# Pairwise-added squares ahead of the norm sums, a separate PSUM bank for the last row block, and a later weight split in a five-layer kernel

## What is computed

```
for each layer:
    h = modulate(rmsnorm(x, g0), sh1, sc1)
    x = x + g1 * mixer(h)              # swa, gla, fox, swa, and a mixed attention ("b2") last
    h = modulate(rmsnorm(x, g1_), sh2, sc2)
    x = x + g2 * feed_forward(h)       # width 2816; with a convolution in the last layer
rmsnorm(x, g) = x * rsqrt(mean(x * x) + 1e-6) * g
```

## Time and profile before

| | |
|---|---|
| median of 3 runs | 1724.33 us (1722.63 to 1727.8) |
| the profiled execution's own time | 1730.59 us |
| its span, first to last instruction | 1728.8 us |
| TensorE matmul busy | 1604.8 us, 93% |
| VectorE busy | 1199.9 us, 69% |
| ScalarE busy | 788.2 us, 46% |
| GpSimd busy | 87.8 us, 5% |
| mean granted TensorE clock | 0.972 |

### The profile page before, as it was taken

How to read it: one execution, slowest core, us unless ns; L and a number is a source line. 1 busy time by engine, 2 the same in 40 slices (tenths; PEclk the granted TensorE clock), 3 DMA queues, 4 the chain that set the end, 5 groups by cost and what they waited for, 6 DMA issues and landing times.

```text
span 1728.8 us, 30748 instructions
## 1 busy us (share of the span) xinstructions
PE 1604.8 (93%) x12542; PEld 1524.9 (88%) x12542; DVE 1199.9 (69%) x1592; ACT 788.2 (46%) x1030; POOL 87.8 (5%) x105
## 2 busy tenths in 40 slices
PE   0878999999899999999999999879999989999998
PEld 0767999999789999998899999858999989889998
DVE  4897777776557777775377777856877778566665
ACT  1453433345534343444454344545434467755453
POOL 0032000000000000001100000020000002300000
PEclk9988999999889999999999999999999999999999
DMA  8755488855324978762339876422987745345550
GB/s 327 301 209 209 199 338 310 321 201 181 116 76 197 385 292 315 267 220 100 144 124 387 307 298 244 183 98 98 365 315 291 295 138 176 123 151 180 185 181 33
DMA packets 54219, 383.75 MB, mean 222 GB/s; under 512 B 6256, under 2 KB 6512, under 8 KB 8448
## 3 DMA queue, kind: packets, MB, share of 16 engines
q1 hardware_dynamic: 50400, 363.75, 56.0%
q0 software_dynamic: 3744, 18.94, 3.1%
HBM read 378.47 MB, written 4.19 MB: 221 GB/s over the span
## 4 chain that ended last, share of the span: by engine, by line
PE 86%; DVE 8%; DMA 2%; ACT 2%; issue 1%; POOL 1%; SPq 0%; DVEq 0%; ACTq 0%
PE PS L1647 71%; PE PS L1668 4%; PE PS L1694 2%; DVE wlo L1173 2%; PE PS L1767 2%; DMA adar<-ada 2%; DVE adar L1187 1%; PE PS L1793 1%; ACT whi L779 1%; DVE XN L1225 1%; PE PS L1814 1%; DVE NM L1330 1%; DVE SCR L1324 1%; DMA raw<-weights 1%; PE PS L1770 1%
## 5 line engine op out<-in xcount | busy, mean ns | idle before, releaser
L1647 PE MATMUL PS<-hhi,whi 128*128 128x256 f32 x2568 | 744.2, 290 | 26.6 <-DVE hlo L1218 23.5
L1647 PE MATMUL PS<-hlo,whi 128*128 128x256 f32 x2568 | 735.8, 287 | 0.0
L1173 DVE TENSOR_TENSOR wlo<-raw,whi 128x2048 fp32r<-128x2048 f32 x234 | 537.0, 2295 | 286.2 <-ACT whi L779 286.1
L1647 PE MATMUL PS<-hhi,wlo 128*128 128x256 f32 x2568 | 735.2, 286 | 0.0
L779 ACT ACTIVATE whi<-raw 128x2048 fp32r<-128x2048 f32 x234 | 446.5, 1911 | 509.8 <-PE PS L1647 481.8
L1647 PEld LDWEIGHTS PS<-hhi,whi 128*128 128x128 f32 x2568 | 502.8, 196 | 43.7 <-issue 40.2
L1647 PEld LDWEIGHTS PS<-hlo,whi 128*128 128x128 f32 x2568 | 503.1, 196 | 1.3 <-issue 1.2
L1647 PEld LDWEIGHTS PS<-hhi,wlo 128*128 128x128 f32 x2568 | 502.3, 196 | 0.0
L1187 DVE CUSTOM_DVE_ANT_0 adar<-adar,CB 128x1024 f32<-128x1024 f32 x240 | 286.4, 1233 | 13.4 <-DMA adar<-ada 13.3
L1647 PE MATMUL PS<-ahi,whi 128*128 128x256 f32 x936 | 265.9, 284 | 1.1 <-DVE alo L1605 1.1
L1647 PE MATMUL PS<-alo,whi 128*128 128x256 f32 x936 | 265.4, 284 | 0.0
(11 more groups left out here) (214 smaller groups left out, 1343.3 us busy)
## 6 DMA issues: line engine op xcount, KB each, us to landing
raw<-weights SPq DMA_DIRECT2D x234, 1024.0 KB, 6.3
adar<-ada SPq DMA_DIRECT2D x108, 1024.0 KB, 5.8
adar<-ada POOLq DMA_DIRECT2D x12, 1024.0 KB, 5.9
bias_rows<-acc POOLq DMA_DIRECT2D x12, 256.0 KB, 3.0
adar<-bias_rows POOLq DMA_DIRECT2D x8, 256.0 KB, 3.3
CST<-cst_in SPq DMA_DIRECT2D x1, 1128.0 KB, 11.7
CB<-c_in SPq DMA_DIRECT2D x2, 512.0 KB, 4.4
X<-x_in SPq DMA_DIRECT2D x1, 1024.0 KB, 8.1
```

The lines of the kernel that those rows point to most:

```text
L1173: v.tensor_tensor(wlo[:, u % CV, :], raw[:, u % RAW, :], whi[:, u % CV, :].bitcast(F32), ALU.subtract).then_inc(lo_done, 1)
L1647: m = pe.matmul(o, w(a), h(b), start=first and k_ == 0, stop=last and k_ == 2, skip_group_check=True)
```

## The change

It does four things. (1) ScalarE squares in five instructions, of two, two, two, one and one row blocks, and the norm's semaphore counts five per norm. (2) After a mixer and after a feed-forward part VectorE adds squares before TensorE sums them: after a mixer five additions put row blocks 0 to 5 into one, and TensorE sums 3 blocks (0, 6, 7); after a feed-forward part three additions put pairs together, and it sums 5 (0, 2, 6, 4, 7). (3) The last row block goes to bank 2, and a signal for block 6 is given before block 7 is multiplied (`out_half` in the out stage, a fourth `y_done` in `down`). Bank 2 is zeroed as a fifth bank before the feed-forward loop. (4) After a feed-forward part `lo` of the next layer's second unit stands behind the updates of x and the additions. In the out stage the splits and ScalarE's three `hi` keep their places; the additions stand between them. The two other norms only get the five squares.

The diff, without the bookkeeping of which norm stands where and the passing of the bank to the out matmuls:

```diff
@@ -250,6 +257,20 @@
         def mixer_ada(l):
             return range(LOOP_ADA[l - 1] + STEPS, LOOP_ADA[l]) if l else range(4, LOOP_ADA[0])
+
+        SQUARES = ((0, 2), (2, 2), (4, 2), (6, 1), (7, 1))
+
+        def adds_to(n):
+
+            return sum({"ffn": 3, "out": 5}.get(plan.place[m], 0) for m in range(n))
+
+        def down_bank(c):
+
+            return bank[4 + c // 2][:, S * (c % 2):S * (c % 2) + S] if c < C - 1 else bank[2][:, 0:S]
+
+        def out_bank(i, t):
+
+            return bank[2][:, 0:S] if (i, t) == (OUT_UNITS - 1, 1) else bank[IB[i]][:, S * t:S * t + S]
         def more_b2(l):
@@ -788,12 +809,12 @@
             def norm(n, l=None, which=0):
-                for q in range(4):
+                for k, w in SQUARES:
                     if n == 0:
                         act.wait_ge(x_in_s, 16)
                     else:
-                        act.wait_ge(x_ready, 8 * (n - 1) + 2 * q + 2)
-                    act.activation(XN[:, 2 * q:2 * q + 2, :], X[:, 2 * q:2 * q + 2, :], ACT.Square).then_inc(norm_sq, 1)
+                        act.wait_ge(x_ready, 8 * (n - 1) + k + w)
+                    act.activation(XN[:, k:k + w, :], X[:, k:k + w, :], ACT.Square).then_inc(norm_sq, 1)
                 act.wait_ge(norm_sum, n + 1)
                 root(RB[:, 0, :], RB[:, 1, :], bank[3][:, 0:S], D).then_inc(norm_r, 1)
                 if n != plan.final_norm:
@@ -1208,6 +1229,17 @@
                                        op0=ALU.add, op1=ALU.mult).then_inc(aff_s, 1)
                 v.wait_ge(aff_s, 2 * l + which + 1)
+            added = [0]
+
+            def add_squares(n, a, b, group=None):
+
+                if group:
+                    v.wait_ge(norm_sq, 5 * n + group)
+                else:
+                    v.wait_ge(norm_add, added[0])
+                added[0] += 1
+                v.tensor_tensor(XN[:, a, :], XN[:, a, :], XN[:, b, :], ALU.add).then_inc(norm_add, 1)
+
             def norm(n, l=None, which=0):
@@ -1559,13 +1591,27 @@
                         lo(plan.uout[l] + i + 2)
                     if l == 0 and i == 0:
                         ada_read(9)
-                    v.wait_ge(pe_unit, plan.uout[l] + i + 1)
+                    if i == OUT_UNITS - 1:
+                        add_squares(plan.norm[l] + 1, 4, 5, 3)
+                        add_squares(plan.norm[l] + 1, 0, 4)
+                    else:
+                        v.wait_ge(pe_unit, plan.uout[l] + i + 1)
                     if i == 0:
                         v.wait_ge(ada_mod, ADA_UNITS * l + 5 + 1)
                     for t in range(2):
                         k = 2 * i + t
-                        v.scalar_tensor_tensor(out=X[:, k, :], in0=bank[IB[i]][:, S * t:S * t + S], scalar=MOD[:, 48 * l + 16 + k:48 * l + 17 + k], in1=X[:, k, :],
+                        if i == OUT_UNITS - 1:
+                            if t == 0:
+                                v.wait_ge(out_half, l + 1)
+                            else:
+                                v.wait_ge(pe_unit, plan.uout[l] + i + 1)
+                        v.scalar_tensor_tensor(out=X[:, k, :], in0=out_bank(i, t), scalar=MOD[:, 48 * l + 16 + k:48 * l + 17 + k], in1=X[:, k, :],
                                                op0=ALU.mult, op1=ALU.add).then_inc(x_ready, 1)
+                    if i == 1:
+                        add_squares(plan.norm[l] + 1, 0, 1, 1)
+                    elif i == 2:
+                        add_squares(plan.norm[l] + 1, 2, 3, 2)
+                        add_squares(plan.norm[l] + 1, 0, 2)
                 affine(l, 1)
                 norm(plan.norm[l] + 1, l, 1)
@@ -1627,16 +1673,24 @@
                         act_lo(1 + st, add=i)
                         if more:
                             ada_add(a0 + st + 2 * i, st, 4 * a0 + 4 * st + 8 * i)
-                if more:
-                    lo(plan.uin[l + 1] + 1)
+                n = plan.norm[l + 1] - (kinds[l + 1] == "b2") if more else None
                 for k in range(8):
                     if k < 6:
-                        v.wait_ge(y_done, 3 * l + k // 2 + 1)
+                        v.wait_ge(y_done, 4 * l + k // 2 + 1)
+                    elif k == 6:
+                        v.wait_ge(y_done, 4 * l + 4)
                     else:
                         v.wait_ge(pe_unit, f + FFN_UNITS)
-                    v.scalar_tensor_tensor(out=X[:, k, :], in0=bank[4 + k // 2][:, S * (k % 2):S * (k % 2) + S], scalar=MOD[:, 48 * l + 40 + k:48 * l + 41 + k],
+                    v.scalar_tensor_tensor(out=X[:, k, :], in0=down_bank(k), scalar=MOD[:, 48 * l + 40 + k:48 * l + 41 + k],
                                            in1=X[:, k, :], op0=ALU.mult, op1=ALU.add).then_inc(x_ready, 1)
+                    if more and k == 3:
+                        add_squares(n, 0, 1, 1)
+                    elif more and k == 5:
+                        add_squares(n, 2, 3, 2)
+                if more:
+                    add_squares(n, 4, 5, 3)
+                    lo(plan.uin[l + 1] + 1)
         @block.tensor
@@ -1668,6 +1722,8 @@
                                 m = pe.matmul(o, hs[x][:, c, P * t:P * t + P], wt(a), start=(c == 0 and k_ == 0), stop=(c == C - 1 and k_ == 2))
                         else:
                             m = split_product(o, lambda a: wt(a)[:, P * t:P * t + P], lambda x: hs[x][:, c, :], c == 0, c == C - 1)
+                    if out == OUT_UNITS - 1 and t == 0:
+                        m.then_inc(out_half, 1)
                 m.then_inc(pe_unit, 1)
             def project_pair(u, before):
@@ -1688,9 +1744,16 @@
             def sum_squares(n):
-                for c in range(C):
-                    if c % 2 == 0:
-                        pe.wait_ge(norm_sq, 4 * n + c // 2 + 1)
+                parts = {"ffn": (0, 2, 6, 4, 7), "out": (0, 6, 7)}.get(plan.place[n], range(C))
+                for c in parts:
+                    if c in (6, 7):
+                        pe.wait_ge(norm_sq, 5 * n + c - 2)
+                    elif plan.place[n] == "ffn":
+                        pe.wait_ge(norm_add, adds_to(n) + c // 2 + 1)
+                    elif plan.place[n] == "out":
+                        pe.wait_ge(norm_add, adds_to(n) + 5)
+                    elif c % 2 == 0:
+                        pe.wait_ge(norm_sq, 5 * n + c // 2 + 1)
                     m = pe.matmul(bank[3][:, 0:S], ones, XN[:, c, :], start=(c == 0), stop=(c == C - 1))
                 m.then_inc(norm_sum, 1)
@@ -1990,13 +2053,15 @@
                 if kind == "gla":
                     project_pair(plan.uout[l], lambda c: pe.wait_ge(o_lo, 8 * l + c + 1))
                     for i in range(2, OUT_UNITS):
-                        project(plan.uout[l] + i, IB[i])
+                        project(plan.uout[l] + i, IB[i], out=i)
                 else:
                     for i in range(2, OUT_UNITS):
                         unit_ready(plan.uout[l] + i)
                         for t in range(2):
                             for p in range(PAIRS):
-                                m = mixed_part(plan.uout[l] + i, p, IB[i], t, p == 0, p == PAIRS - 1)
+                                m = mixed_part(plan.uout[l] + i, p, out_bank(i, t), t, p == 0, p == PAIRS - 1)
+                            if i == OUT_UNITS - 1 and t == 0:
+                                m.then_inc(out_half, 1)
                         m.then_inc(pe_unit, 1)
                 sum_squares(plan.norm[l] + 1)
@@ -2023,17 +2088,17 @@
                     unit_ready(u, add)
                     pe.wait_ge(alo_done, STEPS * l + s_ + 1 + 2 * add)
                     for c in range(C):
-                        o = bank[4 + c // 2][:, S * (c % 2):S * (c % 2) + S]
+                        o = down_bank(c)
                         for t in range(2):
                             m = split_product(o, lambda a: ws[a][:, u % CV, D * t + P * c:D * t + P * c + P],
                                               lambda x: acts[x][:, s_ % 2, S * t:S * t + S], False, True)
-                        if s_ == STEPS - 1 and c % 2 and c < C - 1:
+                        if s_ == STEPS - 1 and c in (1, 3, 5, 6):
                             m.then_inc(y_done, 1)
                     m.then_inc(pe_unit, 1)
                 project_pair(f, before)
-                for b in range(4, 8):
+                for b in (4, 5, 6, 7, 2):
                     pe.matmul(bank[b][:], zeros[:], zeros[:, 0:1].to_broadcast([16, 512]), start=True, stop=True)
                 with pe.Fori(0, 5) as i:
                     for st in range(2):
```

More of the change, by code:

```diff
@@ L107, in __init__ @@
         self.norms = n
+        self.place = {m: "ffn" if m else "load" for m in range(n)}
+        for k, m in zip(kinds, self.norm):
+            self.place[m + 1] = "out"
+            if k == "b2":
+                self.place[m] = "scaled"
     def split_norm(self, n):
@@ L217, in program @@
         norm_h, norm_hi, norm_lo = sem("norm_scaled"), sem("norm_hi"), sem("norm_lo")
```

(11 more changed lines are left out.)

## The result

The changed kernel took 1744.59 us (median of 4 runs, 1741.45 to 1747.22); the kernel before took 1726.07 in 4 runs beside them. The ratio is 1.0104, 95% interval 1.0087 to 1.0122: 18.5 us slower. The direction was forecast, the size was not: +9.7 us, and a range that ended at 1741.3.

The account below looks back on a forecast made before the run. The prediction took TensorE as the bound (86% of the span), the sum itself bounding the out stage. Stall +12.5, clock +2.5, feed-forward ends -6.0, bank +1.1 and end -0.4 gave +9.7 us, 1734.0 us, range 1727.8 to 1741.3.

Parts of the forecast that it names:

- The stall in the out stage: VectorE's first addition waits 3.9 us for the first square; Ln 2.50 us later, +12.5 us over five stages.
- the first addition isn't held: Rival, out stage: squares ready when VectorE reaches the addition; -1.9 us in each stage, 1709.6 us in all; 6%.
- The feed-forward end: Ends of feed-forward parts: earlier updates and a shorter sum bring Ln forward, -1.5 us four times, -6.0 us.
- The small terms: Fifth zeroed bank on TensorE costs +1.1 us over five times; update 6 beside block 7 at program's end saves 0.4.
- TensorE's clock in that gap: Out stage: after idling, TensorE sums blocks 6 and 7 at the low clock; 0.5 us each, +2.5 over five stages.
- The Trainium skill's rule: Out stage: an idle gap halves TensorE's rate, so 0.65 us due in every stage, 3.3 us in place of 2.5.
- The sum: Whole kernel: +12.5 + 2.5 - 6.0 + 1.1 - 0.4 = +9.7 us, giving 1734.0 us.
- the clock makes it dearer: Rival, out stages: low clock covers the sum and a further stretch at the pair of units; +18.2, 1742.5 us; 9%.

Follow-up runs that it names:

- e4: Changed kernel with eight more float32 matmuls of constants ahead of each out stage's sum, where TensorE was idle; 1738.80 us, ratio 1.0069 to before.
- e8: Changed kernel with eight matmuls of constants ahead of each out stage's sum and four behind every norm's sum; 1724.76 us, ratio 0.9978 to before.
- e1: Changed kernel with ScalarE squaring row blocks 0 to 3 ahead of its third hi in the out stage; 1722.39 us, ratio 0.9976 to before.
- e9: e7 with four matmuls of constants behind every norm's sum; 1715.20 us, ratio 0.9917 to before.
- e6: Kernel before with four matmuls of constants behind every norm's sum, nothing else; 1716.01 us, ratio 0.9929 to before.
- e2: Changed kernel without the five out-stage additions, TensorE summing all 8 blocks there; 1728.22 us, ratio 1.0001 to before.
- e3: Changed kernel with the old feed-forward ends: no additions there, 8 blocks summed, split ahead of the updates; 1750.74 us, ratio 1.0139 to before.
- e5: e1 with four matmuls of constants behind every norm's sum; 1707.30 us, ratio 0.9874 to before.
- e7: Changed kernel without any addition, 8 blocks summed everywhere; separate bank, five squares and moved split stay; 1729.17 us, ratio 0.9990 to before.

## Why the prediction was wrong in size

- **The stall in the out stage: right, in place and size.** Forecast was a first addition held for 3.9 us; it was 3.92. Updates 6 and 7 were put at 175.3 and start 11.9 us behind updates 2 and 3, as the working had it (175.26 - 163.31 = 11.95; 173.79 - 161.88 = 11.91). The 2.50 us for each stage are 2.57 with the clock held (e4, e8).
- **Rival "the first addition isn't held": what e1 is.** It gave -1.9 in each stage; measured from the same matmul it is 2.35 against 3.78, -1.43. The working had update 7 start 0.32 us behind the start of the last matmul (171.33 - 171.01), with update 6 done before. In e1 the additions keep VectorE until 166.74, 0.20 behind that start, and update 6 comes first, so update 7 is some 0.3 late; the rest lies between its square and Ln.
- **The feed-forward end: right.** -1.5 was forecast, -1.54 is the distance. The split runs in the gap at 373.75 to 376.0, and VectorE goes on at 376.24, where TensorE's sum and not the split was the limit.
- **The small terms: right.** They are +1.1 and -0.4 of the ledger, and e9 against e6 agrees with their sum: 0.8 us apart with 0.7 by the rows. No run takes them apart.
- **"TensorE's clock in that gap" is the step that failed.** It had two errors. First its size at the sum: I took four instructions at 0.379 us, +0.5 in a stage. All six stand on the path, since block 0, too, waits for the last addition, and at a granted 0.50 the six take 2.94 us against 1.97: +0.97, 4.8 us for five stages instead of 2.5. The price itself was an average of two levels: in the sum of the earlier trace rows the first ten instructions start 0.43 us apart and the last ones 0.22, and in the changed kernel's sums they start 0.43 apart. The Trainium skill's rule of that step would have had the low clock due in every stage. The trace agrees (0.50 in the stretch of the sum, in all five), only the price was higher.
- **The other error of that step: nothing for low stretches behind the feed-forward ends.** A shorter sum is also less work for TensorE there: ten instructions in place of sixteen, and the gap behind them unchanged. By the count over the profiles (16 of 16 places against 6 of 12) two more of the four ends have a low stretch, at 1.3 to 1.5 us each (the 96 matmuls behind them take 12.74 to 12.96 us from first to last start, against 11.46), some 3 us. In e2, where this part stands alone, low clock rose from 84 to 93 us.
- **What the clock came to.** With both gaps filled (e8) the changed kernel is 8.7 us above its counterpart e6, against 18.5 without: 10 of the 18.5 us are clock, for which I had 2.5. The sums are 4.8 of them and the ends some 3; the last 2 have no place in the profiles and are within what the medians leave open.
- **The sum.** +7.2 without the clock term was forecast, and +8.7 measured with the clock held. The rival "the clock makes it dearer" had the right cause and 1742.5 us, at 9%, and the range stopped short of it. But its place was half wrong, so its number is partly luck: it put a further low stretch on the pair of units in each out stage. In the profiles those five pairs take 65.8 us before and 64.4 in the changed kernel, from first to last start. The low stretch there was indeed there already; what grew stands in the sums and behind the ends.

What stays open: how the low stretches split over the stages in an average run, since each kernel has one profile. One case shows how a single profile can mislead. The gla layer's time between its two norms' Ln rose by 8.4 us in the profile of the changed kernel, with a distance that explains 3.5. Another 1.5 are the 96 matmuls at its start, and the last 3.4 are half of a low stretch of 6.8 us inside the mixer, at 504.7 to 511.5. Such a stretch stands there in e2, e3, e4, e5, e7 and e9 as well, two of which have no additions, and not in before, e1, e6 and e8, two of which have them. So it isn't the additions that bring it.

## What to carry to other kernels

When a helper operation is put between two steps of an in-order engine, find in the other engine's written order what its input stands behind: here one wait held two unrelated splits and four updates, and moving two squares ahead of one `hi` turned +1.0% into -0.2%. A sum that is made shorter on TensorE can gain less than its rows say, because TensorE then works less between the same gaps: price the clock with the idle time, and try a few matmuls of constants in a gap before counting a gain in rows. Read the mean granted clock of every run beside its time, or one profile's luck is taken for an effect.

## What was not expected of the hardware

- The time at the low clock differs much between runs of one kernel: 69 to 93 us in 22 runs of the kernel before, with 1721.29 to 1731.53 us of time. Time and low clock go together, with a correlation of 0.8 in these runs, and of 0.6 and 0.8 in two further sets of 13.
- The feed-forward part of the change, 5.7 us by its rows, brought nothing that shows by itself (e2), though every one of its ends was as short as worked out.
- Eight float32 matmul instructions (four matmuls) of useless work behind each norm took 0.7% off the kernel before (1716.01 us, ratio 0.9929), and 0.9% off e1.
